# Seven norms of a fused kernel: earlier diagonals, another order in the first tile pair, constant products, split column sums

## The reference, cut to what matters

```python
def rms_norm(x, g):
    return x * lax.rsqrt(jnp.mean(x * x, axis=-1, keepdims=True) + EPS) * g

# first_block, for each of 2 layers
h = rms_norm(x, norm1_g[l]) * (1.0 + scale1) + shift1
proj = einsum('bsd,dk->bsk', h, w_in[l])            # q, kv latents, rope, conv_u
mix = einsum('bsk,kd->bsd', concat([attention(proj), conv_group(proj)]), w_out[l])
x = x + gate1 * mix
h2 = rms_norm(x, norm2_g[l]) * (1.0 + scale2) + shift2
x = x + gate2 * expert_choice_ffn(h2, w_router[l], w_gate[l], w_up[l], w_down[l])

# second_block, one layer
proj = einsum('bsd,de->bse', rms_norm_2(h, mix_norm_w), w_in)
h = h + einsum('bse,ed->bsd', concat([hgrn2_mix(proj), rglru_mix(proj)]), w_out)
gate, up = split(einsum('bsd,df->bsf', rms_norm_2(h, ffn_norm_w), w_gate_up), 2)
h = h + einsum('bsf,fd->bsd', silu(gate) * up, w_down)
return rms_norm_2(h, final_norm_w)
```

## Time and profile before

| | us |
|---|---|
| median of 3 runs | 3821.96 (3818.45 to 3829.11) |
| the profiled execution | 3824.6 |
| its span | 3822.8 |
| PE busy | 3546.7 |
| VectorE busy | 2424.9 |
| ScalarE busy | 1610.4 |
| GpSimd busy | 971.3 |

### The profile page before, as it was taken

One profiled execution on the slowest core, in us unless ns is written; L12 is line 12 of the kernel. 1 busy time (PEld: TensorE's weight loads), 2 busy tenths in 40 slices (PEclk: granted clock), 3 DMA queues, 4 the chain that ended last, 5 costly groups with the idle time before them and its releaser, 6 DMA issues. The chain is left out here.

```text
span 3822.8 us, 46733 instructions
## 1 busy us (share of the span) xinstructions
PE 3546.7 (93%) x16600; PEld 2846.0 (74%) x16600; DVE 2424.9 (63%) x2262; ACT 1610.4 (42%) x1642; POOL 971.3 (25%) x599
## 2 busy tenths in 40 slices
PE   6997988899999799799889999989986999999998
PEld 6746975688888674697568888868875878888886
DVE  5977776789889597777678888964047232122224
ACT  5124442588888511444258888833134010000001
POOL 0213300011111021330001111125434354454532
PEclk9998999899999899899989999989997989999998
DMA  4100037899999210003789999931100211111101
GB/s 165 44 14 13 13 132 259 293 399 397 392 392 392 92 43 14 13 12 133 267 301 393 402 395 393 389 129 49 45 9 11 77 66 55 38 60 38 58 35 55
DMA packets 128049, 619.18 MB, mean 162 GB/s; under 512 B 17760, under 2 KB 27360, under 8 KB 78816
## 3 DMA queue, kind: packets, MB, share of 16 engines
q1 hardware_dynamic: 119040, 585.65, 40.0%
q0 software_dynamic: 8928, 32.51, 3.2%
HBM read 572.49 MB, written 40.89 MB: 160 GB/s over the span
## 5 line engine op out<-in xcount | busy, mean ns | idle before, releaser
L1868 DVE TENSOR_TENSOR ex_lo<-ex_raw,ex_hi 128x2048 fp32r<-128x2048 f32 x380 | 863.1, 2290 | 124.5 <-ACT ex_hi L1807 124.3
L1807 ACT CAST ex_hi<-ex_raw 128x2048 fp32r<-128x2048 f32 x380 | 724.3, 1914 | 160.6 <-PE psum L1741 144.2
L1739 PE MATMUL psum<-ex_hi,xe_hi 128*128 128x512 f32 x1024 | 403.9, 394 | 1.3 <-DVE xe_lo L1873 1.3
L1741 PE MATMUL psum<-ex_hi,xe_lo 128*128 128x512 f32 x1024 | 400.9, 391 | 0.0
L1740 PE MATMUL psum<-ex_lo,xe_hi 128*128 128x512 f32 x1024 | 400.5, 391 | 0.0
L2613 DVE TENSOR_TENSOR ff_full<-psum,ff_full 128x1024 f32<-128x1024 f32 x22 | 26.9, 1225 | 408.4 <-PE psum L448 408.4
L533 DVE SCALAR_TENSOR_TENSOR mix<-y,lcols,mix 128x1024 f32<-128x1024 f32 x176 | 268.2, 1525 | 5.7
L1739 PEld LDWEIGHTS psum<-ex_hi,xe_hi 128*128 128x128 f32 x1024 | 193.6, 189 | 41.4 <-issue 2.1
L448 PE MATMUL psum<-hn_hi,up_hi 128*128 128x512 f32 x704 | 218.1, 391 | 6.8 <-DVE hn_lo L1966 6.7
L1741 PEld LDWEIGHTS psum<-ex_hi,xe_lo 128*128 128x128 f32 x1024 | 193.3, 189 | 40.9
L1740 PEld LDWEIGHTS psum<-ex_lo,xe_hi 128*128 128x128 f32 x1024 | 193.6, 189 | 39.5
(11 more groups left out here) (445 smaller groups left out, 7424.5 us busy)
## 6 DMA issues: line engine op xcount, KB each, us to landing
ex_raw<-w_experts_dram SPq DMA_DIRECT2D x384, 1024.0 KB, 7.8
mix<-w_ada_dram SPq DMA_DIRECT2D x64, 512.0 KB, 4.3
up_raw<-w_gate_up_dram SPq DMA_DIRECT2D x44, 512.0 KB, 3.3
rt_ada<-w_ada_dram SPq DMA_DIRECT2D x32, 512.0 KB, 6.9
in_raw<-w_in_dram SPq DMA_DIRECT2D x24, 512.0 KB, 3.4
p_raw<-w_in_dram SPq DMA_DIRECT2D x24, 512.0 KB, 3.4
wd_raw<-w_down_dram SPq DMA_DIRECT2D x11, 1024.0 KB, 5.5
ada_w<-w_ada_dram SPq DMA_DIRECT2D x8, 1024.0 KB, 13.6
```

The source lines that it names most:

```text
L1739: pe.matmul(bank(out), x_hi, h[:, k, :], start=first, stop=False)
L1741: mm = pe.matmul(bank(out), x_lo, h[:, k, :], start=False, stop=end)
L1807: act.copy(hi[j % PARTS][:], raw[j % RAW][:]).then_inc(w_hi, 1)
L1868: dve.tensor_tensor(lo[j % PARTS][:], raw[j % RAW][:], hi[j % PARTS][:].bitcast(F32), ALU.subtract).then_inc(w_lo, 1)
```

## The change

- `rstd_pe` takes both square buffers and a count `adds`. It sums `sq_sum` as soon as `adds` additions are there, and then each later square by itself. After the experts `adds` is 5, so there are three sums; elsewhere it is 6, with two sums as before. VectorE's `add_square(n)` stands straight behind the add of tile n in `conv_norm_and_mix`, `mix_out` and `feed_forward`; after the experts it keeps its place, and the last of them goes.
- In `conv_norm_and_mix` the last `reduce_mod` moves behind the sums, and `rstd_dve` ahead of the tensor that waits for it.
- `keep_warm` issues float32 matmuls of constants, 128 by 128 by 512, whose result is never read.
- `project` and `route` make the diagonals first.
- `first_products` takes the place of the two parts in `linear` and of `first_up`: k is the outer loop, each k does hi by hi and lo by hi for both tiles once the activation's high part is there, then hi by lo for both once its low part is there.

```diff
@@ setup, tensor
+                        keep_warm(pe, 2, 2)
+                        rstd_pe(pe, r, psum[:, 0, 0:TB], x_sq, sq_done, sq_added, DT - 2)
+                        keep_warm(pe, 2, 1)
@@ helpers
-        def rstd_pe(pe, r, col, last_sq, sq_done, sq_added):
-            pe.wait_ge(sq_added, DT - 2)
-            token_sums(pe, col, sq_sum)
-            pe.wait_ge(sq_done, DT)
-            token_sums(pe, col, last_sq, False).then_inc(r["summed"], 1)
+        def rstd_pe(pe, r, col, sq, sq_done, sq_added, adds):
+            pe.wait_ge(sq_added, adds)
+            mm = token_sums(pe, col, sq_sum)
+            for n in range(adds + 1, DT):
+                pe.wait_ge(sq_done, n + 1)
+                mm = token_sums(pe, col, sq[n % 2], False)
+            mm.then_inc(r["summed"], 1)
+        def keep_warm(pe, at, n):
+            for _ in range(n):
+                pe.matmul(bank(at), ones, const[:, 0:HALF], start=True, stop=True)
-        def spread_dve(dve, t):
+        def diagonals_dve(dve, t):
             for b in range(TB):
                 dve.tensor_scalar(t["diag"][:, b, :], ident, t["rstd"][:, b:b + 1], None,
                                   ALU.mult).then_inc(t["diag_done"], 1)
+        def spread_dve(dve, t):
+            diagonals_dve(dve, t)
             dve.wait_ge(t["spread_done"], 1)
+        def first_products(pe, outs, w, x_hi, x_lo, K, hi_done, lo_done):
+            for k in range(K):
+                pe.wait_ge(hi_done, k + 1)
+                for b, out in enumerate(outs):
+                    if k == 0:
+                        pe.wait_ge(w["split"][b], 3)
+                        pe.wait_ge(w["read"][b], 1)
+                    for wt in (w["hi"][b], w["lo"][b]):
+                        for half in range(2):
+                            pe.matmul(bank(out + half), wt[:, k, :], x_hi[:, k, half * HALF:(half + 1) * HALF],
+                                      start=k == 0 and wt is w["hi"][b], stop=False)
+                pe.wait_ge(lo_done, k + 1)
+                for b, out in enumerate(outs):
+                    for half in range(2):
+                        mm = pe.matmul(bank(out + half), w["hi"][b][:, k, :], x_lo[:, k, half * HALF:(half + 1) * HALF],
+                                       start=False, stop=k == K - 1)
+                    if k == K - 1:
+                        mm.then_inc(w["done"][b], 1)
@@ linear
-            for part in range(2):
-                for b in range(2):
-                    if part == 0:
-                        pe.wait_ge(w["split"][b], 3)
-                        pe.wait_ge(w["read"][b], 1)
-                    for k in range(part * K // 2, (part + 1) * K // 2):
-                        pe.wait_ge(inputs, k + 1)
-                        mm = products(pe, 4 * b, w["hi"][b][:, k, :], w["lo"][b][:, k, :], x_hi[:, k, :], x_lo[:, k, :],
-                                      k == 0, k == K - 1)
-                    if part:
-                        mm.then_inc(w["done"][b], 1)
+            first_products(pe, (0, 4), w, x_hi, x_lo, K, hi_done, inputs)
@@ project, vector (route the same, without the columns)
+                        diagonals_dve(dve, t)
                         dve.wait_ge(cols_in, 16)
...
-                        spread_dve(dve, t)
+                        dve.wait_ge(t["spread_done"], 1)
@@ project and project2, tensor
+                        keep_warm(pe, 6, 2)
                         spread_pe(pe, t)
-                        linear(pe, h_hi, h_lo, DT, w, IN_TILES // 2, h_ready)
+                        keep_warm(pe, 6, 2)
+                        linear(pe, h_hi, h_lo, DT, w, IN_TILES // 2, h_ready, hi_done)
@@ conv_norm_and_mix, tensor
-                            for c in [c for c in range(1, LATE_CHUNKS) if ends[n - 2] < (c + 1) * DT <= ends[n - 1]]:
+                            for c in [c for c in range(1, LATE_CHUNKS - 1) if ends[n - 2] < (c + 1) * DT <= ends[n - 1]]:
                                 reduce_mod(c)
-                        rstd_pe(pe, r, var_cols, sq[:, (DT - 1) % 2, :], x_sq_done, x_sq_added)
+                        rstd_pe(pe, r, var_cols, [sq[:, b, :] for b in range(2)], x_sq_done, x_sq_added, DT - 2)
+                        reduce_mod(LATE_CHUNKS - 1)
+                        keep_warm(pe, 2, 1)
@@ mix_out; feed_forward the same with keep_warm(pe, 4, 1)
-                        rstd_pe(pe, r, sum_cols, sq[:, (DT - 1) % 2, :], sq_done, sq_added)
+                        rstd_pe(pe, r, sum_cols, [sq[:, b, :] for b in range(2)], sq_done, sq_added, DT - 2)
+                        keep_warm(pe, 6, 1)
...
-                            if n >= 2:
-                                add_square(n - 1)
+                            if 1 <= n < DT - 1:
+                                add_square(n)
@@ run_experts, tensor and vector
+                        rstd_pe(pe, r, sum_cols, [sq[:, b, :] for b in range(2)], sq_done, sq_added, DT - 3)
+                        keep_warm(pe, 7, 2)
...
-                            if n >= 2:
+                            if 2 <= n < DT - 1:
                                 add_square(n - 1)
```

More of the change, by code:

```diff
@@ L450, in products, with linear @@
             return mm
-        def linear(pe, x_hi, x_lo, K, w, pairs, inputs, between=None):
+        def first_products(pe, outs, w, x_hi, x_lo, K, hi_done, lo_done):
[16 more added lines that the diff above has]
+                        mm.then_inc(w["done"][b], 1)
+        def linear(pe, x_hi, x_lo, K, w, pairs, inputs, hi_done):
             for b in range(2):
                 pe.sem_inc(w["done"][b], 1)
-            for part in range(2):
-                if part and between is not None:
-                    between()
-                for b in range(2):
-                    if part == 0:
-                        pe.wait_ge(w["split"][b], 3)
-                        pe.wait_ge(w["read"][b], 1)
-                    for k in range(part * K // 2, (part + 1) * K // 2):
-                        pe.wait_ge(inputs, k + 1)
-                        mm = products(pe, 4 * b, w["hi"][b][:, k, :], w["lo"][b][:, k, :], x_hi[:, k, :], x_lo[:, k, :],
-                                      k == 0, k == K - 1)
-                    if part:
-                        mm.then_inc(w["done"][b], 1)
+            first_products(pe, (0, 4), w, x_hi, x_lo, K, hi_done, inputs)
             with pe.Fori(1, pairs) as i:
@@ L2012, in _ @@
                     def _(pe):
+                        keep_warm(pe, 6, 2)
                         spread_pe(pe, t)
-                        linear(pe, xn_hi, xn_lo, DT, w, n_pairs, lo_done)
+                        keep_warm(pe, 6, 2)
+                        linear(pe, xn_hi, xn_lo, DT, w, n_pairs, lo_done, hi_done)
                     @block.scalar
@@ L2527, in _ @@
                     def _(pe):
-                        def first_up():
-                            for part in range(2):
-                                for b, out in ((0, gate_banks), (1, up_banks)):
-                                    if part == 0:
-                                        pe.wait_ge(w["split"][b], 3)
-                                        pe.wait_ge(read[b], 1)
-                                    for k in range(part * DT // 2, (part + 1) * DT // 2):
-                                        pe.wait_ge(lo_done, k + 1)
-                                        mm = products(pe, out, w["hi"][b][:, k, :], w["lo"][b][:, k, :], hn_hi[:, k, :],
-                                                      hn_lo[:, k, :], k == 0, k == DT - 1)
-                                    if part:
-                                        mm.then_inc(done[b], 1)
                         def up(g, tiles=range(G)):
@@ L2569, in _ @@
                         spread_pe(pe, t)
-                        first_up()
+                        keep_warm(pe, 6, 2)
+                        first_products(pe, (gate_banks, up_banks), w, hn_hi, hn_lo, DT, hi_done, lo_done)
                         up(0, range(1, G))
@@ L2577, in _ @@
                         down(last, lambda part, j: part[:, G * (last % 2) + j, :], 2 * last + 2 * G + 1, last_down["hi"], last_down["lo"])
-                        rstd_pe(pe, r, sum_cols, full[:, (DT - 1) % 2, :], sq_done, sq_added)
+                        rstd_pe(pe, r, sum_cols, [full[:, b, :] for b in range(2)], sq_done, sq_added, DT - 2)
+                        keep_warm(pe, 4, 1)
                     @block.scalar
@@ L2628, in add @@
                                 dve.tensor_tensor(x[:, o, :], banks(down_banks[b]), x[:, o, :], ALU.add).then_inc(down_read[b], 1)
-                                if square and o >= 2:
-                                    add_square(o - 1)
+                                if square and 1 <= o < DT - 1:
+                                    add_square(o)
                         dve.sem_inc(read[1], 1)
```

12 lines of the change are left out of this document (5 added, 7 removed).

## The result

The changed kernel takes 3863.81 us (median of 4 runs, 3860.07 to 3865.89), the kernel before 3822.27 us (4 runs); the ratio is 1.0106 with a 95% interval of 1.0088 to 1.0123. So it is 41.5 us slower. The forecast was 3852 us, +30.2; the median lies 0.8 us above the upper end of the range (3863).

The account below looks back on a forecast made before the run. PE, busy for 93% of the span, was taken as the bound, in `project` VectorE's first multiply; the terms summed to +30.2 us on 3824.6, giving 3854.8, or 3852 on the median's footing; range 3827 to 3863 (8 in 10).

Parts of the forecast that it names:

- The refill: `project2`, `mix_out`, `feed_forward`: releases two matmuls apart leave GpSimd's refill uncovered, +4.4 us each, +13.2 us.
- rival 2: Second pair's refill mostly covered, as GpSimd is quicker or releases further apart; 13.2 + 6.0 drop to some 3: 3836; 10%.
- The clock behind the holes: After the new holes in `project2`, `mix_out` and `feed_forward`, PE runs at low clock: 2.0 us each, +6.0 us.
- The first pair: PE waits for the second tile's low part after four matmuls: `project2` +1.5, `mix_out` +5.0, `feed_forward` +1.9, +8.4 us.
- Constant products at a block's end: After the experts, two products (2.9 us) and the third sum (0.7) start the next block late: +3.6 us in `project2`.
- rival 1: At every crossing the constant products keep the clock high, so not slower: -4.3 us, 3818; 15%.
- The sums: After `mix_out` the first sum runs behind the products, -3.1 us, -2.0 with its constant; before each router +0.3.
- The end of `feed_forward`: Final adds 3.6 us apart where PE needs 2.72: +2.5 us, with the constant +1.1, +3.6 before the final norm.
- `project`: Earlier first pair frees 2.6 us a layer, less a late h_hi (0.3, 1.7): -2.3 and -0.9 us.
- I cost it at nothing: In `project` the refill hole costs nothing: VectorE has 16 taps to do, needs the next pair some 28 us later.
- rival 3: VectorE does not cover the holes in `project`; longer refill or clock loss adds 2 to 4 us a layer: 3858; 10%.
- The release ahead of ScalarE's cast: In `project` constant products precede the increment letting ScalarE split the first tile: nothing, up to 3.4 us if it waited.

Follow-up runs that it names:

- The spread releases: Changed kernel with k outermost for k 0 to 3 only, then k 4 to 7 tile by tile, so the first tile is released earlier: 3843.7 us, ratio 1.0052.
- The short low parts: Changed kernel, but behind the first pair of `project` GpSimd writes 8 columns of a low part instead of 1024, leaving out computation: 3846.6 us (one run).
- the old additions: Changed kernel with `feed_forward`'s additions of squares again one tile behind the add: 3854.8 us (one run).
- The last version: Kernel before plus split sums (`mix_out`, router), diagonals first, three sums in `feed_forward`; old first pair, no constant products, two sums after experts: 3816.7 us, ratio 0.9986.

## Why the forecast was right, and where it was short

Added up, the order of the first pair costs 27.4 us alone and 31.7 in the changed kernel, the constant products 12.9 alone and 13.7. The two alone make 40.3 of the 41.5 us. By their intervals the order alone lies between 18 and 31 us and the constants between 8 and 17, so what is left of the change could be a gain or a loss of some us; parts of it gain. The causes and the direction were forecast; the terms came out 10 us short in sum (+30.2 against the 40.5 between the two profiled spans), as read below.

**The refill.** Forecast: 4.85 us idle for 0.45 at three places, 13.2 us. Measured: 5.39 for 0.45, 5.06 for 0.13 and 4.99 for 0.05, 14.8 us. The forecast had taken the gap of the weight load in the earlier trace rows for an idle PE. The spread releases take it away, so the mechanism is shown: rival 2 is out.

**The clock behind the holes.** Forecast 2.0 each, 6.0 us; measured 5.85/2, 3.28/2 and 4.00/2 = 6.6 us, and 6.8 us come back when the holes are filled.

**The first pair.** It waits, as forecast, for the second tile's low part after four matmuls. PE's timeline of `project2`:

```profile
2550.68 1.19 PE L477 MATMUL psum<-xn_hi,p_hi 128*128 128x512 f32 x2 [4.25 <-issue]
...
2551.67 1.06 PE L477 MATMUL psum<-xn_hi,p_lo 128*128 128x512 f32 x2
...
2556.78 1.22 PE L477 MATMUL psum<-xn_hi,p_hi 128*128 128x512 f32 x2 [4.05 <-POOL p_lo L430]
```

The pair ends 38.4 us after the first diagonal in `project2`, 36.9 before: +1.6 for +1.5. In `mix_out`, from its first matmul, it takes 29.4 us for 24.8: +4.6 for +5.0. In `feed_forward` 39.9 for 35.9: +3.9 for +1.9. There GpSimd's first split, which waits for the transfer of its weights, began 4.50 us after the first diagonal, 2.97 before; with the order alone it was 2.95 again and the pair +1.9 late, as forecast. In the other runs with the new order the split began after 2.8 to 3.2 us, so the other 2.0 us are this execution's later transfer, not the order.

**Constant products at a block's end.** Behind the last experts, the constants, the reciprocal and the next block's diagonals:

```profile
2535.68 3.76 PE L374 MATMUL psum<-const 128*128 128x512 f32 x4
...
2536.07 0.20 DVE L384 RECIPROCAL rstd<-cb_root 128x8 f32<-128x8 f32 x1 [9.36 <-ACT cb_root L379]
...
2540.93 2.11 DVE L391 TENSOR_SCALAR mix<-const,rstd 128x128 f32<-128x128 f32 x8
```

and the instructions of the barrier, ns:

```profile
L1699 PEldq DRAIN  x2: 6748/6748/6748, 1288.4 to 2532.7; - x2
...
L1699 DVEq DRAIN  x2: 235/236/237, 1291.7 to 2536.1; - x2
```

DRAIN lasts 6.75 us (4.0 in the earlier trace rows) and ends at 2539.5, just as the last constant does; that is 3.2 us after VectorE's reciprocal. From the last product to the first diagonal are 18.9 us for 14.8: +4.1, forecast +3.6. The Trainium skill (TensorE: Matmul & The Clock Gate, section Why this matters for your kernels) advises against idle stretches between bursts. The holes agree with it (filled, they kept 1.00). The page does not say that filler matmuls pay, and at the block ends they did not: 12.9 us were lost with the constants alone, so rival 1 is out. The mean granted clock was 0.953 before and 0.952 with the constants alone. At most crossings the idle time behind the constants, for the spread, the activations and the weights, was still there, and the low stretch moved without vanishing.

**The sums.** `mix_out`: forecast -2.0 with its constant, measured -2.4 (6.8 us from the last product to the first diagonal for 9.2). The first sum follows the products at full clock:

```profile
3080.97 1.84 PE L351 MATMUL psum<-const,sq_sum 128*128 128x1 f32 x16
...
3083.53 1.95 PE L351 MATMUL psum<-const,so_sq 128*128 128x1 f32 x16 [0.73 <-ACT so_sq L1371]
...
3085.34 1.87 PE L374 MATMUL psum<-const 128*128 128x512 f32 x2
```

Ahead of the router (forecast +0.3 each) the last product and the first diagonal are 0.6 and 1.4 us further apart than before. PE in layer 0:

```profile
614.45 1.84 PE L351 MATMUL psum<-const,sq_sum 128*128 128x1 f32 x16
...
617.08 3.03 PE L351 MATMUL psum<-const,cn_sq 128*128 128x1 f32 x16 [0.79 <-ACT cn_sq L1337]
...
619.97 3.55 PE L205 MATMUL psum<-const,cn_diag 128*128 128x1 f32 x16
...
623.38 2.06 PE L374 MATMUL psum<-const 128*128 128x512 f32 x2
```

The two sums end 4.0 us sooner after the last product, and the reduction, now at the low level (3.55 for 1.84 in the earlier trace rows), and the constant give it back, since the DRAIN waits for both.

**The end of `feed_forward`.** Forecast +3.6. DVE's adds and additions, then PE:

```profile
3825.97 1.22 DVE L2650 TENSOR_TENSOR x<-psum,x 128x1024 f32<-128x1024 f32 x1
...
3828.31 1.23 DVE L2643 TENSOR_TENSOR sq_sum<-sq_sum,ff_full 128x1024 f32<-128x1024 f32 x1 [1.13 <-ACT ff_full L2624]
...
3829.46 1.22 DVE L2650 TENSOR_TENSOR x<-psum,x 128x1024 f32<-128x1024 f32 x1
...
3830.73 0.73 PE L461 MATMUL psum<-ff_hid_hi,up_hi 128*128 128x512 f32 x2 [0.48 <-DVE x L2650]
...
3836.56 3.57 PE L351 MATMUL psum<-const,sq_sum 128*128 128x1 f32 x16 [2.81 <-DVE sq_sum L2643]
...
3839.99 3.55 PE L351 MATMUL psum<-const,ff_full 128*128 128x1 f32 x16
```

The adds are 3.49 us apart (forecast 3.6), PE loses 1.9 us over its waits for them, and from the last product to the first diagonal are 12.0 us for 10.1: +3.8 together.

**`project`: here a term was missing.** Forecast -2.3 and -0.9, measured -1.1 in layer 0 (first sum of the next block 216.36 for 217.42) and +2.3 in layer 1 (+1.25 there, -1.0 at the first diagonal). Two steps were off. `h_hi` was not one of them: it came 0.5 us early in layer 0 (forecast 0.3 late) and 0.8 late in layer 1 (forecast 1.7). The first multiply came 28.1 and 28.0 us after h_hi, 29.4 before: 1.3 us for the 2.6 of the forecast. PE ended the pair at 90.62, as worked out (90.5), but both tiles end together now, so ScalarE's table load and sigmoid, which ran beside the second tile before, stand behind it (90.27 to 92.59). And "I cost it at nothing" failed, though not by rival 3: VectorE covered the holes in PE (5.5 us), with no gap over 0.15 us from the first multiply to the last tap of layer 0. The taps' row of the page (268.2 us, mean 1525 ns before), and GpSimd and VectorE behind the first multiply:

```profile
L556 DVE SCALAR_TENSOR_TENSOR mix<-y,lcols,mix 128x1024 f32<-128x1024 f32 x176 | 274.4, 1560 | 5.7
...
93.67 5.66 POOL L448 TENSOR_TENSOR in_lo<-in_raw,in_hi 128x1024 fp32r<-128x1024 f32 x2 [25.87 <-ACT in_hi L439]
...
93.99 9.06 DVE L556 SCALAR_TENSOR_TENSOR mix<-y,lcols,mix 128x1024 f32<-128x1024 f32 x4
```

While GpSimd makes a low part a tap takes 3.1 to 3.5 us, not 1.3. Before, part of the first refill lay in the time in which VectorE waited for PE; now all of it lies over taps. That is 3.1 us a layer (112.85 for 109.78 of taps), more than the gain at the multiply. That layer 0 still came out 1.1 us ahead is because PE's last tiles and ScalarE's copy of them ended the stage before (213.8), and VectorE's last tap ends it now (212.7); that the forecast for layer 0 came out within 1.2 us is luck. The short low parts show that GpSimd's work is the cause. The Trainium skill (GPSIMD Engine Reference, section 8. Key points) says that GpSimd shares its SBUF interfaces with VectorE and contends with VectorE instructions that have two SBUF inputs; a tap has two (y and mix), and the trace agrees. The forecast should have drawn on it. `project` (4.4 us) and the late first pair of `feed_forward` (2.0) are 6.4 of the 10 us by which the sum fell short; the rest is 2.2 us in refill and clock, 1.4 at the routers and 0.5 behind the experts, less 0.5 in the other terms. Unedited stages differ by up to 2.5 us either way between the two profiled executions, and come out near nothing together.

**The release ahead of ScalarE's cast** was costed at nothing. That was right: the cast waits for the transfer.

**Open.** That the clock falls 2.6 us after the last product of `feed_forward` in the kernel before, and 4.9 us after it with the old additions, was seen and not explained; it moves the sums by 2 us from run to run. The last version gained 10.1 us between the profiled executions and 5.4 in the medians: the profiled execution before (3824.6) lies 2.5 us above its median, that of the last version (3814.5) 2.2 below. What makes one execution slower than another no trace here shows.

## What to carry to other kernels

When a loop has one buffer for each tile of a pair, the time between the two releases is what hides the refill; an order that finishes both tiles together ends with an empty pipe, however well it starts. Work put into an engine's idle time is free only if nothing waits for that engine to drain: ahead of a barrier it is on the path at once, while inside a hole that stays anyway it kept the clock. And work that moves from beside a waiting engine to beside a working one is not free, even on another engine.

## What the runs showed of the hardware

- A float32 tap of VectorE (128 by 1024, two operands and a column) took 1.29 us with GpSimd idle, and 3.1 to 3.5 us when GpSimd's subtraction (2.4 us alone) ran beside it. In the kernel before that makes some 17 us of taps a layer (109.8 for 92.5); what the stage itself would gain is less, 7.0 us in layer 0 of the changed kernel.
- Five constant products (4.45 us) in a hole of 5 us kept the granted clock at 1.00 behind it at all three places; unfilled, it was 0.50 for 3.3 to 5.9 us.
- A column sum of 16 records took 1.84 us right behind dense products; after a wait of 2.8 us it took 3.57, after one of 2.45 us 1.95 in one run. In `feed_forward` three sums that started at once ended 6.05 us after the last product, two that waited 9.30 us after it.
